# The modulation matrix of an encoder layer: a third of it loaded and multiplied ahead of the projections, the rest in two bursts inside attention

## What is computed

```
mod = silu(c) @ w_ada + b_ada                      # w_ada is 1024 x 6144, float32: 24 MB
sh1, sc1, g1, sh2, sc2, g2 = split(mod, 6)
u   = layer_norm(x) * (1 + sc1) + sh1              # needs the first two parts of mod only
h   = u @ w_in                                     # then q, k, v of 8 GQA heads and 8 MLA heads
o   = attention(h)                                 # 16 heads
x   = layer_norm(alpha*x + g1 * (norm(o) @ w_out)) # needs part 3
u2  = layer_norm(x) * (1 + sc2) + sh2              # parts 4 and 5
y   = layer_norm(alpha*x + g2 * ffn(u2))           # part 6
```

## Time and profile before

| | |
|---|---|
| median of 3 runs | 1982.06 us (1980.81 to 1983.81) |
| the profiled execution | 1981.43 us, its span 1979.6 us |
| granted TensorE clock, mean | 0.963 |
| busy: PE, DVE, ACT, POOL | 1807.0, 1163.6, 697.9, 210.2 us |
| moved | 171.56 MB, mean 87 GB/s |
| `w_ada_ring` loads | 12 of 2048 KB, median 12.5 us to landing |

### The profile page before, as it was taken

One profiled execution on the slowest core, in us unless ns is written; L12 is line 12 of the kernel. 1 busy time (PEld: TensorE's weight loads), 2 busy tenths in 40 slices (PEclk: granted clock), 3 DMA queues, 4 the chain that ended last, 5 costly groups with the idle time before them and its releaser, 6 DMA issues. The chain is left out here.

```text
span 1979.6 us, 22389 instructions
## 1 busy us (share of the span) xinstructions
PE 1807.0 (91%) x8558; PEld 1395.8 (71%) x8558; DVE 1163.6 (59%) x1406; ACT 697.9 (35%) x1081; POOL 210.2 (11%) x218
## 2 busy tenths in 40 slices
PE   7989896399999999679979999999999999999993
PEld 1188885266667777467768888888888888888873
DVE  1268887488887777359854434434444434444488
ACT  1145654277776766534431111111111111111114
POOL 0012333111022221000000000000000000000053
PEclk9989997699999999889989999999999999999997
DMA  9913435713155543143241111111111111111133
GB/s 348 323 57 91 133 108 157 173 46 77 46 120 135 123 105 80 47 138 107 75 128 32 33 42 32 32 53 32 32 42 32 32 53 32 32 42 32 34 105 128
DMA packets 145001, 171.56 MB, mean 87 GB/s; under 512 B 21434, under 2 KB 108506, under 8 KB 144930
## 3 DMA queue, kind: packets, MB, share of 16 engines
q1 hardware_dynamic: 130352, 121.72, 19.7%
q0 software_dynamic: 12016, 46.22, 9.3%
q10 hardware_dynamic: 2564, 2.72, 0.5%
HBM read 128.22 MB, written 42.32 MB: 86 GB/s over the span
## 5 line engine op out<-in xcount | busy, mean ns | idle before, releaser
L1796 DVE TENSOR_TENSOR sum_f<-pair,sum_f 128x1024 f32<-128x1024 f32 x200 | 244.1, 1221 | 468.5 <-PE pair L160 466.8
L158 PE MATMUL pair<-u_hi,w_out_hi 128*128 128x512 f32 (+1 forms) x1056 | 377.0, 357 | 12.2 <-DVE w_out_hi L1424 12.2
L160 PE MATMUL pair<-u_hi,w_out_hi 128*128 128x512 f32 (+1 forms) x1056 | 374.9, 355 | 0.0
L159 PE MATMUL pair<-u_lo,w_out_hi 128*128 128x512 f32 (+1 forms) x1056 | 372.4, 353 | 0.0
L1644 ACT ACTIVATE silu_gate<-pair 128x512 f32<-128x512 f32 (+1 forms) x63 | 33.2, 526 | 574.9 <-PE pair L160 574.9
L158 PEld LDWEIGHTS pair<-u_hi,w_out_hi 128*128 128x128 f32 x1056 | 199.1, 189 | 40.0 <-DVE w_out_hi L1424 12.4
L160 PEld LDWEIGHTS pair<-u_hi,w_out_hi 128*128 128x128 f32 x1056 | 199.0, 188 | 31.1
L159 PEld LDWEIGHTS pair<-u_lo,w_out_hi 128*128 128x128 f32 x1056 | 198.7, 188 | 30.4
L1123 DVE TENSOR_TENSOR p_lo<-p_f,p_hi 128x1024 fp32r<-128x1024 f32 (+1 forms) x144 | 167.2, 1162 | 43.4 <-ACT p_hi L1088 42.9
L158 PE MATMUL pair<-down_hi,hidden_hi 128*128 128x512 f32 x440 | 183.2, 416 | 9.6 <-DVEq L1767 6.1
L1084 ACT ACTIVATE p_f<-pair 128x1024 f32<-128x1024 f32 (+1 forms) x144 | 140.6, 977 | 141.9 <-PE pair L984 69.4
(11 more groups left out here) (236 smaller groups left out, 2935.0 us busy)
## 6 DMA issues: line engine op xcount, KB each, us to landing
w_ada_ring<-in_w_ada SPq DMA_DIRECT2D x12, 2048.0 KB, 12.5
gate_up_raw<-in_w_gate SPq DMA_DIRECT2D x21, 512.0 KB, 4.0
gate_up_raw<-in_w_up SPq DMA_DIRECT2D x21, 512.0 KB, 5.2
down_raw<-in_w_down SPq DMA_DIRECT2D x21, 512.0 KB, 3.2
o<-o_head POOLq DMA_DIRECT2D x16, 320.0 KB, 3.6
o_tile<-o SPq DMA_DIRECT2D x10, 512.0 KB, 4.1
x<-y SPq DMA_DIRECT2D x10, 512.0 KB, 2.6
gate_up_raw<-x SPq DMA_DIRECT2D x10, 512.0 KB, 3.6
```

The lines of the kernel that those rows point to most:

```text
L158: pe.matmul(out, a[0], b[0], start=start, stop=False)
L159: pe.matmul(out, a[0], b[1], start=False, stop=False)
L160: return pe.matmul(out, a[1], b[0], start=False, stop=stop)
L1796: dve.tensor_tensor(sumf[:, t, :], src, sumf[:, t, :], ALU.add).then_inc(dn_added, 1)
```

## The change

Only the first 4 of the 12 chunks are now multiplied ahead of the projections, each in a buffer of its own. SP issues chunks 0 and 1, then the two `x` tiles, then chunks 2 and 3, none with a wait. The two result rows no longer go through memory: TensorE transposes them into columns (`columns`) and VectorE copies these to `mod_in_t`. VectorE's order is three splits, one bias add, three splits, and so on.

The other 16 MB of `w_ada` are read in attention, into the SBUF that `w_out_hi` and `w_out_lo` take later: POOL issues four loads of 2 MB (rows of 8 KB) behind the loads of heads 1 and 2, and four more once `store(2)` is issued. TensorE multiplies each half in one go at (head 3, unit 2) and (head 7, unit 2): 32 matmuls, each with 32 stationary columns (two vectors and 30 columns of zeros) and 512 moving ones, matmul q writing to partitions 32q to 32q+31 of `A_PAIR`. VectorE adds the bias on all 128 partitions (`late_sum`), SP stores four pairs of rows. SP also clears the semaphores of the first two stages, some 60, between `load_first` and the first maxima row, since attention's new ones need the numbers.

```diff
+            k.wo_at = -(-nc.sbuf_base // 32) * 32
             k.wo = [k.sb(weights, "w_out_hi", [P, KT, D], F32R), k.sb(w_out_lo_memory, "w_out_lo", [P, KT, D], F32R)]
             with ExitStack() as stage:
                 attention(k, stage)
+            first_sems.close()
...
-    NC = 6 * D // 512
-    RING = 3
+    NC = 2 * D // 512
     right = lambda name, shape: k.sb(stage, name, shape, side="right")
     c_t = right("c_t", [P, KT, 2])
-    silu_c = right("silu_c", [P, KT, 2])
-    wa = right("w_ada_ring", [P, RING, KT, 512])
-    bias = right("b_ada_rows", [2, 6 * D])
-    mrow = right("mod_chunk", [2, 2, 512])
+    wa = right("w_ada_first", [P, NC, KT, 512])
+    bias = right("b_ada_rows", [2, 2 * D])
+    mrow = right("mod_chunk", [2, NC, 512])
     raw = right("w_raw", [P, 2, W_IN])
...
+    def load_first(sp, n):
+        sp.dma_start(wa[:, n, :, :], k.wada[:, :, n * 512:(n + 1) * 512]).then_inc(wa_in[n], 16)
+
+    k.load_w_ada = load_first
...
-        wsrc = k.i["w_ada"][0].rearrange("(p j) n -> p j n", j=KT)
-        for n in range(NC):
-            if n >= RING:
-                sp.wait_ge(mod_done, n - RING + 1)
-            sp.dma_start(wa[:, n % RING, :, :], wsrc[:, :, n * 512:(n + 1) * 512]).then_inc(wa_in[n % RING], 16)
+        for n in range(2):
+            load_first(sp, n)
...
+        def columns(n):
+
+            pe.wait_ge(mod_sum, n + 1)
+            for q in range(4):
+                at = 2 * (4 * n + q)
+                mm = pe.transpose(bank(k, 7)[:, at:at + 2], mrow[:, n, q * P:(q + 1) * P], k.ident[0:2, 0:2])
+            mm.then_inc(k.mod_tr, 1)
+
         pe.wait_ge(c_ready, 1)
+        pe.wait_ge(ident_in, 16)
         for n in range(NC):
-            pe.wait_ge(wa_in[n % RING], 16 * (n // RING + 1))
-            if n >= 8:
-                pe.wait_ge(mod_sum, n - 7)
+            pe.wait_ge(wa_in[n], 16)
             for j in range(KT):
-                mm = pe.matmul(bank(k, n % 8)[0:2, :], silu_c[:, j, :], wa[:, n % RING, j, :],
-                               start=j == 0, stop=j == KT - 1)
+                mm = pe.matmul(bank(k, n)[0:2, :], k.silu_c[:, j, 0:2], wa[:, n, j, :], start=j == 0, stop=j == KT - 1)
             mm.then_inc(mod_done, 1)
+            if n >= 1:
+                columns(n - 1)
+        columns(NC - 1)
...
-        assert len(pieces) <= NC
-        for n in range(NC):
-            if n < len(pieces):
-                act.wait_ge(raw_in[n % 2], 16 * (n // 2 + 1))
-                hi = pieces[n][1]
-                act.activation(hi, raw[:, n % 2, :hi.shape[-1]], ACT.Copy).then_inc(hi_done, 1)
-            if n >= 1:
-                act.wait_ge(mod_sum, n)
-                act.dma_start(k.mod[:, (n - 1) * 512:n * 512], mrow[:, (n - 1) % 2, :]).then_inc(mod_out[(n - 1) % 2], 16)
-        act.wait_ge(mod_sum, NC)
-        act.dma_start(k.mod[:, (NC - 1) * 512:], mrow[:, (NC - 1) % 2, :]).then_inc(mod_out[(NC - 1) % 2], 16)
+        act.wait_ge(c_zero, 1)
+        act.activation(k.silu_c[:, :, 0:2], c_t[:, :, :], ACT.Silu).then_inc(c_ready, 1)
+        for n, (src, hi, lo) in enumerate(pieces):
+            act.wait_ge(raw_in[n % 2], 16 * (n // 2 + 1))
+            act.activation(hi, raw[:, n % 2, :hi.shape[-1]], ACT.Copy).then_inc(hi_done, 1)
...
+        done = 0
         for n in range(NC):
-            if n < len(pieces):
-                split(n)
+            for m in range(done, min(done + 3, len(pieces))):
+                split(m)
+            done += 3
             dve.wait_ge(mod_done, n + 1)
             if n == 0:
                 dve.wait_ge(b_in, 16)
-            if n >= 2:
-                dve.wait_ge(mod_out[n % 2], 16 * (n // 2))
-            dve.tensor_tensor(mrow[:, n % 2, :], bank(k, n % 8)[0:2, :], bias[:, n * 512:(n + 1) * 512], ALU.add).then_inc(mod_sum, 1)
-        for m in range(NC, len(pieces)):
+            dve.tensor_tensor(mrow[:, n, :], bank(k, n)[0:2, :], bias[:, n * 512:(n + 1) * 512], ALU.add).then_inc(mod_sum, 1)
+        for m in range(done, len(pieces)):
             split(m)
 
...
         eng.wait_ge(k.lo_done, k.pieces)
-        for s in range(2):
-            eng.wait_ge(k.mod_out[s], 16 * (6 * D // 512 // 2))
+        eng.wait_ge(modp, 2)
...
-        for s in range(2):
-            sp.wait_ge(k.mod_out[s], 32)
-        with nc.allow_non_contiguous_dma(reason="modulation columns, once"):
-            for s in range(2):
-                for m, part in enumerate((1, 0)):
-                    sp.dma_start(modt[:, s, m, :], k.mod[s, part * D:(part + 1) * D].rearrange("(j p) -> p j", p=P)).then_inc(mod_in, 16)
         for t in range(2):
             sp.dma_start(xt[:, t, :], xrow(k, t)).then_inc(x_in[t], 16)
+        for n in (2, 3):
+            k.load_w_ada(sp, n)
...
-        dve.wait_ge(mod_in, 64)
-        for s in range(2):
-            m = dve.tensor_scalar(modt[:, s, 0, :], modt[:, s, 0, :], 1.0, None, ALU.add)
-            if s == 0:
-                link(m)
-        m.then_inc(modp, 1)
+        dve.wait_ge(k.mod_tr, 4)
+        cols = bank(k, 7)[:, 0:4 * KT].rearrange("p (m j s) -> p m s j", m=2, s=2)
+        dve.tensor_copy(modt[:, :, 1, :], cols[:, 0, :, :]).then_inc(modp, 1)
+        dve.tensor_scalar(modt[:, :, 0, :], cols[:, 1, :, :], 1.0, None, ALU.add).then_inc(modp, 1)
...
+    FIRST, HALF = 2 * D, 2 * D
+    late_w = nc.alloc_sbuf_tensor_at("w_ada_late", [P, KT, HALF], F32, offset=k.wo_at)
+    late_bias = sb("b_ada_late", [P, 2, 512])
+    late_row = sb("mod_late", [P, 2, 512])
+    late_in, late_b_in, late_out = k.sem("late_in"), k.sem("late_b_in"), k.sem("late_out")
+    LATE_AT = {(3, 2): 0, (7, 2): 1}
...
+            for done in k.first:
+                sp.sem_clear(done)
 
             for g in range(H):
                 sp.wait_ge(m_row, g + 1)
                 row = qs[1][DA:DA + 1, g % RING, :] if gqa(g) else qs[0][DM:DM + 1, g % RING, :]
                 sp.dma_start(row.bitcast(F32), mrow[:, :].bitcast(F32)).then_inc(m_in, 16)
+                for (late_g, _), half in LATE_AT.items():
+                    if late_g == g:
+                        sp.wait_ge(a_free, late_use(half) + 1)
+                        for q in range(4):
+                            at = FIRST + HALF * half + 512 * q
+                            sp.dma_start(k.mod[:, at:at + 512], late_row[32 * q:32 * q + 2, half, :]).then_inc(late_out, 16)
+            sp.wait_ge(late_out, 16 * 8)
...
+            link(pool.memset(late_bias[:, :, :], 0.0))
+            for q in range(4):
+                for half in range(2):
+                    at = FIRST + HALF * half + 512 * q
+                    pool.dma_start(late_bias[32 * q:32 * q + 2, half, :], k.i["b_ada"][0, at:at + 512].partition_broadcast(2)).then_inc(late_b_in, 16)
+            def load_late(half):
+
+                at = FIRST + HALF * half
+                for j in range(0, KT, 2):
+                    pool.dma_start(late_w[:, j:j + 2, :], k.wada[:, j:j + 2, at:at + HALF]).then_inc(late_in, 16)
+
+            load_late(0)
             for g in range(H):
                 if g + 3 < H:
                     load(pool, g + 3)
                 if HA - 1 <= g < H - 1:
                     load_w_out(g - HA + 1)
                 store(g)
+                if g == 2:
+                    pool.wait_ge(a_ready, late_use(0) + 1)
+                    load_late(1)
...
+            def modulate_late(half):
+                use_before(pe, late_use(half))
+                pe.wait_ge(late_in, 16 * KT // 2 * (half + 1))
+                for j in range(KT):
+                    for q in range(4):
+                        mm = pe.matmul(A_PAIR[32 * q:32 * q + 32, 0, :], k.silu_c[:, j, :], late_w[:, j, q * 512:(q + 1) * 512],
+                                       start=j == 0, stop=j == KT - 1)
+                mm.then_inc(a_ready, 1)
...
+                    if (g, u) in LATE_AT:
+                        modulate_late(LATE_AT[g, u])
...
+                act.wait_ge(a_ready, late_use(1) + 1)
...
+            def late_sum(half):
+
+                dve.wait_ge(a_ready, late_use(half) + 1)
+                dve.wait_ge(late_b_in, 16 * 8)
+                dve.tensor_tensor(late_row[:, half, :], A_PAIR[:, 0, :], late_bias[:, half, :], ALU.add).then_inc(a_free, 1)
```

More of the change, by code:

```diff
@@ L73, in __init__ @@
         self.i, self.o = ins, outs
-        self.names = set()
+        self.sems, self.first = ctx, []
     def sem(self, name):
-        return self.ctx.enter_context(self.nc.semaphore(name))
+        found = self.sems.enter_context(self.nc.semaphore(name))
+        if self.sems is not self.ctx:
+            self.first.append(found)
+        return found
     def sb(self, stage, name, shape, dt=F32, side=None):
@@ L92, in encoder_layer @@
         k.eps = k.sb(ctx, "eps", [P, 1])
+        k.silu_c = k.sb(ctx, "silu_c", [P, KT, 32])
         k.mod = k.dram("mod_rows", [2, 6 * D])
@@ L107, in encoder_layer @@
         k.o_sample = lambda t: outs["y_sample"][0, t * P:(t + 1) * P, :]
```

(65 more changed lines are left out.)

## The result

The changed kernel takes 1973.76 us (median of 6 runs, 1972.29 to 1976.58), the kernel before beside it 1982.62 us (6 runs, 1979.64 to 1986.23). The ratio is 0.9956 with a 95% interval of 0.9943 to 0.9969: 0.44% faster. The forecast was 1989 us, slower. The time lies in the range, near what rival B gives (1975.5).

What follows compares the result with a forecast made beforehand. TensorE was taken as the bound in attention, without slack, and all its time ahead of the projections as on the path. -44 + 28 + 20 + 3 = +7 us on the span of 1979.6 gave 1989, range 1968 to 2018.

Steps and rivals of the forecast that it cites:

- rival B: Late products in attention: four column groups run side by side, a block takes 6.9 us, total 1975.5, faster; chance 0.22.
- the length of a late product: Two blocks of 32 matmuls in attention, 13.7 us each, 14.2 with the bias add: +28 us, between 15 and 56.
- The head: Stage before the projections: eight chunks leave, the last splits set its end, fourth add at 54.6 against 98.83: -44 us.
- The first burst: Start of attention: four 2 MB loads in q0 delay head 0's `v` rows and maxima row in q1: +20 us.
- Rival D: The first burst holds nothing back (8 KB rows cut finer or turns by bytes): 1969, with B 1956; chance 0.17.
- The second burst: Loads behind `store(2)` delay `load(6)` and so the first maxima of head 6: +3 us, from 0 to 8.
- Priced at nothing: ScalarE's and SP's row stores, SP's clearing of some 60 semaphores, ScalarE's wait at `w_out_hi`: no cost.
- C: Late products' column groups run one after the other: 2 x 13.8 us more, 2017; chance 0.2.

## Why the prediction was wrong, and where it was right

**The step that failed is the length of a late product.** I took 13.7 us and 14.2 with the add, by the assumption that the second record of a matmul, bound to the same column group, also holds back the first of the next group. The block takes 7.0 us. That is rival B, which I gave 0.22. The lower bound in the sum was right (6.9), and the choice between the bounds was made from the order in the program alone, with no row for it. The runs with other orders show what stands in its place: records of other groups start past those that wait for a busy group, as long as no more than about four of that group are on hand. Nearly all of the error is there. With 7.0 and 0.5 for a block the prediction's own sum is -44 + 15 + 20 + 3 = -6, 1976.0 us on the median's scale, and 1973.8 was measured.

**The head** was right in size and cause: -45.5 for -44, and the last splits did end last, 1 us earlier than I had them. The run with more buffers adds that the chunks' transfers stood right behind, so that this cure alone gives nothing.

**The first burst** was right in its cause and nearly in size: packets one for one (98 and 99), `v_lo` over 35 us to landing, and a wait before `scores(0, 0)` of 18.0 us for 20. That the seam comes to exactly 20.0 is luck: 1.8 us of it are lost in the projections, and they are still lost with the burst moved. Moving the burst shows it as the cause of the rest: 18.3 us in the trace, 17.2 of the time. Rival D (it holds nothing back) is out.

**The second burst** was right: 2.4 us of wait for 3, and 3.4 of time when it is moved. What the prediction did not have is the lower clock behind the wait, which makes up the difference.

**Priced at nothing:** once both bursts are later, TensorE's waits from the seam to the end of attention (330 to 797 us) are those of the kernel before but for 1.3 us in front of the two late products. None is for the cleared semaphores, the row stores or ScalarE's wait at `w_out_hi`.

**A row misread.** The 4.9 us that I called TensorE's largest wait in attention are ten waits together; the longest is 1.3 us. Nothing in the sum hangs on it.

**Rivals C and B.** C (one after the other, 2017) is what the program gets when it is written group after group, and even then only 2005.

## What to carry to other kernels

Before a big transfer is issued early, count the rows that stand in the other queues at that moment, not their bytes: with turns by packets each small row waits for one big packet, and where there are more rows than packets, as here (some 2000 and 1024), they wait for the whole burst. A burst that is wanted much later goes behind the next head's own loads; here two moved lines were worth 20.7 us, more than twice what the whole change had brought. Small products that go to different column groups should be written with the groups in turns: two or four records of one group in a row were free here, eight were not. A short wait of TensorE costs more than its length when the clock falls behind it. And where transfers set a stage, what is not needed first goes behind what TensorE waits for.

## What I had not expected of the hardware

- Four column groups run fully side by side, two float32 records per matmul included: 64 records in 7.0 us, 16 steps of 0.43, where one after the other they would take 27.5 (64 steps, worked out and not run). The Trainium skill, page "TensorE: Matmul & The Clock Gate", Part 3 (packing small matmuls), has three groups at 2.38 times the rate; the trace shows four at 27.5 / 7.0 = 3.9 times.
- A busy column group holds back the others only from about the fifth of its records in a row. A block takes 7.0, 7.15, 15.8 and 22.5 us for runs of 2, 4, 8 and 16 records.
- A wait of 2.35 us was followed by 3.4 us at a granted clock of 0.50, one of 6.4 us by 6.4 us at 0.50.
- Rows of 1 and 2 KB from GpSimd's queue went out in packets of about 4 KB, rows of 8 KB in packets of 8 KB.
